# Pairing VectorE's residual adds in the second half of three RMS borders of a two-block transformer kernel

## The chip, the cores and the metric

The program runs on one core of a Trainium2 chip. The metric is the device time of one execution in microseconds. A core has a matrix engine (TensorE, PE in the profile), a vector engine (VectorE, DVE), an activation engine (ScalarE, ACT), GpSimd (POOL) and a sync engine (SP) that issues transfers. Each has its own instruction stream, and they meet by semaphores. PEld is the weight load that goes with each matmul.

## What is computed

The reference runs three layers over 512 tokens of width 1024, all in float32. What matters here is the residual border between a branch `m` and what follows it, three times in the first block:

```python
def _rms_norm(x, g):
    y = x * lax.rsqrt(jnp.mean(x * x, axis=-1, keepdims=True) + NORM_EPS)
    return y * g

h = h + _rms_norm(m, norm_g[layer, 1])                                     # a border
f = _squared_relu_mlp(_rms_norm(h, norm_g[layer, 2]), ffn_w1[layer], ffn_w2[layer])
h = h + _rms_norm(f, norm_g[layer, 3])                                     # a border
```

The borders in question are the one between the first mixer and the first feed-forward part (`ffn0`), the one between `ffn0` and the second mixer (`sgu_in`), and the one between the second mixer and the second feed-forward part (`ffn1`).

## The kernel before

Activations lie transposed: feature on the 128 partitions, in 8 blocks `k` of 128 features, tokens along the free axis. `h` is the residual stream, `acc` the branch's result, both 128 x 8 x 512 float32. A border works on the tokens in two halves `s` of 256, so that TensorE can go on with one half while the other is being normalised.

Products are made in three passes, for precision: each operand is split into a high part (rounded for the matmul) and a low part (the rest). The high part of the next stage's input, `xa[:, k, 0]`, is made by ScalarE from `h` with the gain of the next norm; the low part, `xa[:, k, 1]`, is made by VectorE from `h` and the high part. The reciprocal root of the next norm is applied later, so TensorE needs only these two.

In the second half (s = 1) of a border, the work for each block k before the change is:

1. VectorE, line 596 (`dve_post_scale`): `acc = acc * gain * rs`, where `rs` lies in a PSUM bank (the reciprocal of line 593). It raises `post_ready`.
2. VectorE, line 601 (`dve_post_add`): waits for `post_ready` of its block, `h = h + acc`. It raises `h_ready`.
3. ScalarE, line 637 (`hi` in `act_boundary`): waits for `h_ready` to reach the block's count, writes the high part of `xa`, raises `pre_hi`.
4. VectorE, line 610 (`lo` in `dve_boundary`): waits for `pre_hi`, writes the low part, raises `pre_lo`.
5. TensorE: at the borders into `ffn0` and `ffn1` line 510 (`pe_quad`), 12 products of 128x256 for each block: four for the high part with the weights' high part, four for the high part with the weights' low part, and then, after a wait for `pre_lo`, four for the low part. At the border into `sgu_in` line 1754 (`v_first`), 6 products of 128x512 for each block, two, two and two in the same order. The high part is waited for with `pre_hi` at each block's first product.

Ahead of block 0 of the second half TensorE runs a few products on constants (line 482, `pe_hold`; 3 at the first and third border, 4 at the second), whose result is not used.

VectorE's order is written out by hand in the table `STEPS`: "rs" is the reciprocal, ("step", k) is scale k, add k, low part k - 1, "last" is low part 7, and "split" is the low part of a weight panel (line 365). ScalarE's order, in `act_boundary`, is high parts 0 to 6, the high part of panel 4, high part 7, and the high parts of panels 5 and 6. Behind the half comes the panel work of the next stage (line 392 at `ffn0` and `ffn1`, line 1766 at `sgu_in`).

Of the kernel before, what the change touches and what calls it, by code (L numbers as in the profile page):

```python
# [24 lines left out]
ALU = mybir.AluOpType  # L25
# [7 lines left out]
KC = D // P  # L33
# [185 lines left out]
def build(nc, stream, x, vec, con, rope, cmp_pos, cmp_w1, cmp_w2, gate_w, w_s, b_s, rpb, mask, out, stop=None):  # L219
    with ExitStack() as ctx:  # L220
        sems = {}

        def sem(name):
            if name not in sems:
                sems[name] = ctx.enter_context(nc.semaphore(name))
            return sems[name]
# [4 lines left out]
        def keep(name, shape, dt=F32):  # L231
            size = int(np.prod(shape[1:])) * (2 if dt == BF16 else 4)
            size = -(-size // 128) * 128
            t = nc.alloc_sbuf_tensor_at(name, shape, dt, offset=place[0])
            place[0] += size
            return t

        h = keep("h", [P, KC, T])
# [9 lines left out]
        rs = keep("rs", [P, T])  # L248
# [13 lines left out]
        def at(name, shape, kb, dt=F32):  # L262
            assert shared + int(kb * 1024) + int(np.prod(shape[1:])) * 4 <= nc.sbuf_usable_end, name
            return nc.alloc_sbuf_tensor_at(name, shape, dt, offset=shared + int(kb * 1024))

        xb = at("xb", [P, KC, 2, T], 0, F32R)
        acc = at("acc", [P, KC, T], 32)
# [69 lines left out]
        def col(table, i=0):  # L337
            return vecs[:, VEC[table] + i:VEC[table] + i + 1]
# [21 lines left out]
        def dve_split(dve, n, more=0):  # L360
            m = n + AHEAD
            if m >= NP:
                return
            dve.wait_ge(hi_done, m + 1 + more)
            nc.vector.tensor_tensor(ring[:, m % RING, 1], raw[:, m % RING], ring[:, m % RING, 0].bitcast(F32),  # L365
                                    ALU.subtract).then_inc(lo_done, 1)
# [59 lines left out]
        def half(s):  # L426
            return slice(HT * s, HT * s + HT)
# [14 lines left out]
        def pe_squares(pe, i):  # L442
# [6 lines left out]
        STEPS = ([("rs", 0), ("step", 0), ("out", 0), ("step", 1), ("split", 0), ("step", 2), ("out", 1), ("step", 3),  # L449
                  ("out", 2), ("out", 3), ("split", 1), ("step", 4), ("step", 5), ("split", 2), ("step", 6), ("split", 3),  # L450
                  ("step", 7), ("last", 0)],
                 [("rs", 1)] + [("step", k) for k in range(8)] + [("last", 1), ("split", 4), ("split", 5), ("split", 6)])

        def tail_base(name):
            return BASE[name] + dict(STAGES)[name] - 4, TAIL_AT[name]
# [135 lines left out]
        def dve_post_rs(dve, chain, r, s):  # L591
            dve.wait_ge(sem("post_sd"), 2 * r + s + 1)
            chain(nc.vector.reciprocal(ps[6 + s][:, half(s)], ps[6 + s][:, half(s)]))

        def dve_post_scale(dve, r, s, k, g):
            nc.vector.scalar_tensor_tensor(out=acc[:, k, half(s)], in0=acc[:, k, half(s)], scalar=col("norm_g", g * KC + k),
                                           in1=ps[6 + s][:, half(s)], op0=ALU.mult, op1=ALU.mult).then_inc(sem("post_ready"), 1)

        def dve_post_add(dve, r, s, k):
            dve.wait_ge(sem("post_ready"), 16 * r + 8 * s + k + 1)  # L600
            nc.vector.tensor_tensor(h[:, k, half(s)], h[:, k, half(s)], acc[:, k, half(s)], ALU.add)\
                .then_inc(sem("h_ready"), 1)

        def dve_boundary(dve, chain, r, g_post, name, g_pre, out):

            u0 = 8 + 16 * r

            def lo(s, k):
                dve.wait_ge(sem("pre_hi"), u0 + 8 * s + k + 1)
                nc.vector.scalar_tensor_tensor(out=xa[:, k, 1, half(s)], in0=h[:, k, half(s)],  # L610
                                               scalar=col("norm_g", g_pre * KC + k),
                                               in1=xa[:, k, 0, half(s)].bitcast(F32), op0=ALU.mult, op1=ALU.subtract)\
                    .then_inc(sem("pre_lo"), 1)

            for q in range(4):
                out(0, q)
            for s in range(2):
                for what, i in STEPS[s]:
                    if what == "rs":
                        dve_post_rs(dve, chain, r, s)  # L620
                    elif what == "step":
                        dve_post_scale(dve, r, s, i, g_post)
                        dve_post_add(dve, r, s, i)
                        if i >= 1:
                            lo(s, i - 1)
                    elif what == "last":
                        lo(s, KC - 1)
                    elif what == "out":
                        out(1, i)
                    else:  # L630
                        dve_split(dve, BASE[name] + i - AHEAD)
# [1718 lines left out]
        def _(dve):  # L2350
# [327 lines left out]
            dve_split(dve, BASE["mix0_nsa"])  # L2678
            dve.wait_ge(taken["act"], READS["act"][BASE["mix0_nsa"]])
            dve_boundary(dve, chain, 0, 1, "ffn0", 2, out_nsa)  # L2680
            dve_ffn(dve, "ffn0")
            dve_boundary(dve, chain, 1, 3, "sgu_in", 4, out_tail("ffn0"))
            for k in range(1, KC):
                dve.wait_ge(sem("pre_sq"), k + 1)
# [90 lines left out]
            for j in range(13):  # L2775
                dve_split(dve, B + j)
                if j % 2 == 1:
                    dve.wait_ge(panel_done, B + j + 1)
                    nc.vector.tensor_copy(acc[:, j // 2], ps[BANK[B + j]][:, :]).then_inc(taken["dve"], 2)
            dve_boundary(dve, chain, 2, 5, "ffn1", 6, out_sgu)  # L2780
            dve_ffn(dve, "ffn1")

# [278 lines left out]
```

## Time and profile before

| what | value |
|---|---|
| time, median of 3 runs | 2045.3 us (2044.89 to 2045.57) |
| the profiled execution's own time | 2045.47 us |
| its span, first to last instruction | 2043.7 us |
| busy: TensorE, VectorE, ScalarE, GpSimd | 99%, 51%, 39%, 8% |
| mean granted TensorE clock | 0.999 of full speed |
| the chain that ended last: TensorE, VectorE, ScalarE | 93%, 4%, 2% |

The profiled execution's time is its span and 1.8 us around it. A share of busy time is a mean over all stages. How the engines stand in one short stretch, such as a border of some 12 us, is read from the timeline of that stretch.

### The profile page before, as it was taken

To read this page: it belongs to the slowest core of one execution; us is meant where nothing else is said; L and a number is where in the kernel's file an instruction comes from. 1 tells how busy PE (TensorE), PEld (TensorE's weight loads), DVE (VectorE), ACT (ScalarE), POOL (GpSimd) and SP (SyncE) were. 2 spreads that over 40 slices of the span, in tenths; PEclk is the share of its full clock that TensorE was granted. 3 is DMA by queue.
4 is the path that set the end of the run, shared out by engine and by line. 5 is a ranking of instruction groups with operands and counts; after the bars stand their busy time and mean duration, and the time that the engine had idled before them with its cause. 6 is when DMAs were issued, how large, how long until landed. Compare 5 with 4: busy or idle time off the path is not lost.

```text
span 2043.7 us, 28848 instructions
## 1 busy us (share of the span) xinstructions
PE 2022.7 (99%) x11240; PEld 1711.4 (84%) x11240; DVE 1048.1 (51%) x1722; ACT 802.4 (39%) x1348; POOL 173.6 (8%) x160
## 2 busy tenths in 40 slices
PE   9999999999999999999999999999999999999998
PEld 7888788888889888889888888987888898888887
DVE  6557867344345736527443434727544545344344
ACT  7326644223233533324332323535554345323232
POOL 1001010100002001210220002300000220000000
PEclk9999999999999999999999999999999999999999
DMA  5222013332322322232333323232122313333321
GB/s 194 89 71 84 22 38 108 93 103 92 97 89 86 120 86 86 87 103 73 104 93 102 98 88 103 83 113 93 44 63 83 103 52 114 93 95 94 99 83 42
DMA packets 52047, 182.12 MB, mean 89 GB/s; under 512 B 5872, under 2 KB 8064, under 8 KB 51936
## 3 DMA queue, kind: packets, MB, share of 16 engines
q1 hardware_dynamic: 50112, 173.23, 27.0%
q0 software_dynamic: 1824, 7.32, 1.0%
q8 instruction: 80, 1.31, 0.3%
q14 instruction: 31, 0.25, 0.0%
HBM read 178.43 MB, written 2.10 MB: 88 GB/s over the span
## 4 chain that ended last, share of the span: by engine, by line
PE 93%; DVE 4%; ACT 2%; issue 0%; DMA 0%; POOL 0%; SPq 0%; ACTq 0%; DVEq 0%
PE ps L392 59%; PE ps L1101 5%; PE ps L471 4%; PE ps L510 3%; PE ps L1766 3%; PE ps L1843 3%; PE ps L1041 2%; PE ps L1084 2%; PE ps L1058 1%; PE ps L1754 1%; PE ps L1486 1%; PE ps L822 1%; PE ps L1464 1%; PE ps L1602 1%; DVE ring L365 1%; PE ps L1856 1%
## 5 line engine op out<-in xcount | busy, mean ns | idle before, releaser
L392 PE MATMUL ps<-xa,ring 128*128 128x512 f32 x3048 | 702.9, 391 | 0.0
L392 PEld LDWEIGHTS ps<-xa,ring 128*128 128x128 f32 x3048 | 570.1, 188 | 120.5 <-issue 2.7
L358 ACT ACTIVATE ring<-raw 128x1024 fp32r<-128x1024 f32 x320 | 336.6, 1054 | 482.2 <-PE ps L392 382.1
L365 DVE TENSOR_TENSOR ring<-raw,ring 128x1024 fp32r<-128x1024 f32 x320 | 402.0, 1259 | 205.5 <-ACT ring L358 205.0
L392 PE MATMUL ps<-xb,ring 128*128 128x512 f32 x2208 | 502.6, 389 | 0.0
L392 PEld LDWEIGHTS ps<-xb,ring 128*128 128x128 f32 x2208 | 414.4, 188 | 86.1
L947 DVE TENSOR_TENSOR ffsq<-relu 128x512 f32<-128x512 f32 x96 | 66.3, 691 | 178.8 <-ACT relu L906 178.8
L964 DVE TENSOR_TENSOR acc<-acc,ps 128x512 f32<-128x512 f32 x68 | 46.8, 688 | 196.3 <-PE ps L392 196.3
L906 ACT ACTIVATE relu<-ps 128x512 f32<-128x512 f32 x64 | 38.1, 596 | 185.0 <-PE ps L392 182.7
L950 DVE TENSOR_TENSOR xb<-ffsq,xb 128x512 fp32r<-128x512 f32 x96 | 66.5, 692 | 75.8 <-ACT xb L898 75.8
L1101 PE MATMUL ps<-xa,ring 128*128 128x512 f32 x432 | 104.3, 396 | 0.0
L510 PE MATMUL ps<-xa,ring 128*128 128x256 f32 x768 | 97.1, 286 | 2.5 <-issue 1.2
L510 PEld LDWEIGHTS ps<-xa,ring 128*128 128x128 f32 x768 | 93.7, 192 | 5.1 <-issue 1.4
L1101 PEld LDWEIGHTS ps<-xa,ring 128*128 128x128 f32 x432 | 79.4, 188 | 18.2
L471 PE MATMUL ps<-xb,ring 128*128 128x256 f32 x576 | 71.6, 285 | 0.0
L471 PEld LDWEIGHTS ps<-xb,ring 128*128 128x128 f32 x576 | 70.3, 192 | 0.5
L1766 PE MATMUL ps<-ring,xa 128*128 128x512 f32 x288 | 65.7, 389 | 0.0
L898 ACT ACTIVATE xb<-ffsq 128x512 fp32r<-128x512 f32 x96 | 59.8, 623 | 10.4 <-DVE ffsq L947 10.3
L1766 PEld LDWEIGHTS ps<-ring,xa 128*128 128x128 f32 x288 | 54.0, 188 | 11.2
L1843 PE MATMUL ps<-yhi,ring 128*128 128x512 f32 x192 | 59.4, 389 | 0.0
L906 ACT ACTIVATE relu<-ps,vecs 128x512 f32<-128x512 f32 x32 | 22.0, 686 | 88.1 <-PE ps L392 86.7
L563 POOL TENSOR_TENSOR part<-part,xf 128x512 f32<-128x512 f32 x8 | 14.4, 1801 | 473.5 <-ACT xf L547 473.5
(371 smaller groups left out, 2061.2 us busy)
## 6 DMA issues: line engine op xcount, KB each, us to landing
raw<-in_stream SPq DMA_DIRECT2D x320, 512.0 KB, 3.5
t<-in_rpb POOLq DMA_DIRECT2D x8, 384.0 KB, 5.6
h<-in_x SPq DMA_DIRECT2D x8, 256.0 KB, 7.1
c_w<-in_cmp_w POOLq DMA_DIRECT2D x4, 512.0 KB, 4.0
out_y<-h SPq DMA_DIRECT2D x16, 128.0 KB, 1.9
cons<-in_con SPq DMA_DIRECT2D x1, 578.0 KB, 8.9
raw<-in_stream SPq DMA_DIRECT2D x2, 256.0 KB, 3.9
wst<-in_w_s POOLq DMA_DIRECT2D x1, 512.0 KB, 3.5
```

The costliest lines, as they stand in the source:

```text
L358: nc.scalar.activation(ring[:, m % RING, 0], raw[:, m % RING], ACT.Copy).then_inc(hi_done, 1)
L365: nc.vector.tensor_tensor(ring[:, m % RING, 1], raw[:, m % RING], ring[:, m % RING, 0].bitcast(F32), ALU.subtract).then_inc(lo_done, 1)
L392: mm = nc.tensor.matmul(bank[:, :], ring[:, n % RING, w, k * P:(k + 1) * P], operand[:, k, xx], start=(start and i == 0 and w == 0 and xx ...
L471: mm = nc.tensor.matmul(ps[bank][:, half(q % 2)], ring[:, n % RING, w, k * P:(k + 1) * P], operand[:, k, xx, half(s)], start=(k == 0 and w ...
L510: mm = nc.tensor.matmul(ps[QUAD[c]][:, half(s)], ring[:, (n0 + k // 2) % RING, w, at_w:at_w + P], xa[:, k, xx, half(s)], start=(k == 0 and ...
L898: nc.scalar.activation(xb[:, j - 1, 0], ffsq[:, (j - 1) % 2], ACT.Copy).then_inc(sem("ff_hi"), 1)
L906: nc.scalar.activation(relu[:, j % 2], ps[at][:, :], ACT.Relu, bias=b).then_inc(taken["act"], 1)
L947: nc.vector.tensor_tensor(ffsq[:, j % 2], relu[:, j % 2], relu[:, j % 2], ALU.mult)\
L950: nc.vector.tensor_tensor(xb[:, j, 1], ffsq[:, j % 2], xb[:, j, 0].bitcast(F32), ALU.subtract).then_inc(sem("ff_lo"), 1)
L1101: mm = nc.tensor.matmul(ps[BANK[n]][:, :], ring[:, n % RING, w, k * P:(k + 1) * P], operand[:, k, xx], start=(k == 0 and w == 0 and xx == ...
L1766: mm = nc.tensor.matmul(ps[V_BANKS[g][t]][:, :], xa[:, k, xx, t * P:(t + 1) * P], ring[:, n % RING, w, (k % 2) * T:(k % 2) * T + T], start ...
L1843: mm = nc.tensor.matmul(ps[BANK[n]][:, :].rearrange("p (t d) -> p t d", t=TB), ring[:, n % RING, w, k * P:(k + 1) * P], y_block(KC * i + k ...
```

## The change

In the second half of each of the three borders, the table now lists ("two", k) for k = 0, 2, 4, 6 in place of the eight ("step", k). A "two" scales blocks k and k + 1, adds both to `h` in one instruction of 128 x 2 x 256 that waits for both scales and raises `h_ready` by 2, and then makes the low parts k - 2 and k - 1, if there are any. "last" of the second half makes low parts 6 and 7. The first half, ScalarE's order and TensorE's order are as they were.

```diff
-                 [("rs", 1)] + [("step", k) for k in range(8)] + [("last", 1), ("split", 4), ("split", 5), ("split", 6)])
+                 [("rs", 1)] + [("two", k) for k in range(0, 8, 2)] + [("last", 1), ("split", 4), ("split", 5), ("split", 6)])
...
+        def dve_post_add_two(dve, r, s, k):
+            dve.wait_ge(sem("post_ready"), 16 * r + 8 * s + k + 2)
+            nc.vector.tensor_tensor(h[:, k:k + 2, half(s)], h[:, k:k + 2, half(s)], acc[:, k:k + 2, half(s)], ALU.add)\
+                .then_inc(sem("h_ready"), 2)
...
+                    elif what == "two":
+                        dve_post_scale(dve, r, s, i, g_post)
+                        dve_post_scale(dve, r, s, i + 1, g_post)
+                        dve_post_add_two(dve, r, s, i)
+                        if i >= 2:
+                            lo(s, i - 2)
+                            lo(s, i - 1)
                     elif what == "last":
+                        if s == 1:
+                            lo(s, KC - 2)
                         lo(s, KC - 1)
```

VectorE at the start of the second half of the first border, before. L596 is the scale, L601 the add, L610 the low part:

```order
L596 SCALAR_TENSOR_TENSOR acc<-acc,vecs,ps 128x256 [waits dve_chain]
L601 TENSOR_TENSOR h<-h,acc 128x256 [waits post_ready]
L596 SCALAR_TENSOR_TENSOR acc<-acc,vecs,ps 128x256
L601 TENSOR_TENSOR h<-h,acc 128x256 [waits post_ready]
L610 SCALAR_TENSOR_TENSOR xa<-h,vecs,xa 128x256 [waits pre_hi]
```

The last three rows repeat for blocks 2 to 7. The same place in the changed kernel, where line 606 is the two-block add and line 615 the low part:

```order
L596 SCALAR_TENSOR_TENSOR acc<-acc,vecs,ps 128x256 [waits dve_chain]
L596 SCALAR_TENSOR_TENSOR acc<-acc,vecs,ps 128x256
L606 TENSOR_TENSOR h<-h,acc 128x2x256 [waits post_ready]
L596 SCALAR_TENSOR_TENSOR acc<-acc,vecs,ps 128x256 x2
L606 TENSOR_TENSOR h<-h,acc 128x2x256 [waits post_ready]
L615 SCALAR_TENSOR_TENSOR xa<-h,vecs,xa 128x256 [waits pre_hi] x2
```

What moved: the first `h` of the half comes after two scales and a two-block add; the first low part comes after four scales and two two-block adds, where it came after two scales and two adds.

TensorE at the same place has the same rows in both kernels, the constants' products and then blocks 0 and 1:

```order
L482 MATMUL ps<-cons 128x256 x3
L510 MATMUL ps<-xa,ring 128x256 [waits pre_hi]
L510 MATMUL ps<-xa,ring 128x256 x7
L510 MATMUL ps<-xa,ring 128x256 [waits pre_lo]
L510 MATMUL ps<-xa,ring 128x256 x3
```

Nothing moved there: a block's first eight products need its high part alone, and the last four need its low part.

## Rows read from the trace of the kernel before

**Rows 1.** The page: granted clock in its 40 slices, and the chain's shares.

```profile
PEclk9999999999999999999999999999999999999999
...
PE 93%; DVE 4%; ACT 2%; issue 0%; DMA 0%; POOL 0%; SPq 0%; ACTq 0%; DVEq 0%
```

**Rows 2.** VectorE's timeline, first border: start, us, engine, line, operation.

```profile
309.97 0.48 DVE L596 SCALAR_TENSOR_TENSOR acc<-acc,vecs,ps 128x256 f32<-128x256 f32 x1
310.49 0.42 DVE L601 TENSOR_TENSOR h<-h,acc 128x256 f32<-128x256 f32 x1
310.83 0.47 DVE L596 SCALAR_TENSOR_TENSOR acc<-acc,vecs,ps 128x256 f32<-128x256 f32 x1
...
311.68 0.48 DVE L610 SCALAR_TENSOR_TENSOR xa<-h,vecs,xa 128x256 fp32r<-128x256 f32 x1
312.07 0.47 DVE L596 SCALAR_TENSOR_TENSOR acc<-acc,vecs,ps 128x256 f32<-128x256 f32 x1
...
313.32 0.48 DVE L596 SCALAR_TENSOR_TENSOR acc<-acc,vecs,ps 128x256 f32<-128x256 f32 x1
```

**Rows 3.** ScalarE's timeline, first border, high parts 0 and 6 and a panel.

```profile
310.94 0.51 ACT L637 ACTIVATE xa<-h,vecs 128x256 fp32r<-128x256 f32 x1 [3.20 <-DVE h L601]
...
318.03 0.51 ACT L637 ACTIVATE xa<-h,vecs 128x256 fp32r<-128x256 f32 x1 [0.73 <-DVE h L601]
318.45 1.04 ACT L358 ACTIVATE ring<-raw 128x1024 fp32r<-128x1024 f32 x1
```

**Rows 4.** TensorE's timeline, first border.

```profile
309.95 1.46 PE L482 MATMUL ps<-cons 128*128 128x256 f32 x6
311.50 11.77 PE L510 MATMUL ps<-xa,ring 128*128 128x256 f32 x96
323.12 13.11 PE L392 MATMUL ps<-xa,ring 128*128 128x512 f32 x57
```

**Rows 5.** VectorE's timeline, second border: scale 0.

```profile
665.70 0.48 DVE L596 SCALAR_TENSOR_TENSOR acc<-acc,vecs,ps 128x256 f32<-128x256 f32 x1
```

**Rows 6.** The chain at the second border: start, us, what.

```profile
667.23 11.19 PE ps L1754 x48
678.42 5.67 PE ps L1766 x25
```

**Rows 7.** The chain at the third border.

```profile
950.39 0.49 DVE acc L596
...
951.93 11.78 PE ps L510 x96
963.71 6.37 PE ps L392 x28
```

**Rows 8.** Adds by line: min/median/max ns, first and last start, forms.

```profile
L601 DVE TENSOR_TENSOR h<-h,acc x48: 424/425/462, 290.0 to 959.2; 128x256 f32<-128x256 f32 x48
...
L540 DVE TENSOR_TENSOR acc<-acc,ps x12: 673/687/689, 635.5 to 2027.1; 128x512 f32<-128x512 f32 x12
```

**Rows 9.** VectorE's timeline in ffn0: an operation of 512 columns and its successor.

```profile
334.22 0.69 DVE L950 TENSOR_TENSOR xb<-ffsq,xb 128x512 fp32r<-128x512 f32 x1 [0.70 <-ACT xb L898]
334.83 1.22 DVE L365 TENSOR_TENSOR ring<-raw,ring 128x1024 fp32r<-128x1024 f32 x1
```

**Rows 10.** Timeline, second border: a low part, and TensorE's load waiting for it.

```profile
662.85 0.48 DVE L610 SCALAR_TENSOR_TENSOR xa<-h,vecs,xa 128x256 fp32r<-128x256 f32 x1
...
663.38 1.67 PEld L1754 LDWEIGHTS ps<-ring,xa 128*128 128x128 f32 x8 [0.19 <-DVE xa L610]
```

**Rows 11.** TensorE's timeline, first border, first half: waits before products.

```profile
295.82 3.58 PE L510 MATMUL ps<-xa,ring 128*128 128x256 f32 x28 [1.21 <-issue]
299.88 1.22 PE L510 MATMUL ps<-xa,ring 128*128 128x256 f32 x8 [0.47 <-DVE ring L365]
```

**Rows 12.** Stretches: us, PE busy (products), granted clock, DMA share, GB/s.

```profile
294.60:302.00 7.40, 5.46 (x40) 1.00 0.32 95
...
311.50:323.20 11.70, 11.70 (x97) 1.00 0.05 6
```

## The prediction, made before the changed kernel ran

> **What bounds the kernel now.** The page comes first. TensorE holds 93% of the chain that ended last, at a granted clock that is full in every slice [rows 1]. Anything that makes TensorE start later lengthens the kernel by as much, unless it would have waited for something else anyway. Next I looked at the stretch that the change touches, the second half of each border, engine by engine on the timeline. VectorE works there with hardly a gap: scale, add, low part, and block 2's scale starts 1.25 us before block 3's (312.07 and 313.32) [rows 2]. TensorE starts that half at 311.50 and then runs 96 products in 11.77 us with no gap up to the next stage [rows 4]. That is 0.1226 us for a product and 1.47 us for a block of 12. So the half has two limits, one after the other. Its start hangs on VectorE and ScalarE: reciprocal, scale 0, add 0, high part 0, first product (311.45 is the high part's end, 311.50 the product's start) [rows 2 to 4]. After the start the limit is TensorE, since a block takes it 1.47 us and VectorE 1.25 us. The other two borders look the same: 48 products in 11.19 us, 0.233 us each, at the second [rows 6], 96 in 11.78 us at the third, where the chain itself goes through scale 0 [rows 7].
>
> **What the change removes.** Four adds in each border's second half. One add of 256 columns takes 0.425 us. One of 512 columns, of the same two-row pattern of 2 x 256 (line 540 addresses two blocks of `acc` like that, with its second input in PSUM), takes 0.687 us [rows 8]. An operation with both inputs in SBUF takes 0.69 us, and its successor starts 0.61 us after it [rows 9]. I take 0.69 us for the pair and 0.61 us to the next start. Between small operations: an unheld one follows a scale or a low part after 0.39 us (311.68 to 312.07), an add follows a scale that it waits for after 0.50 to 0.52 us, and what follows a small add comes after 0.34 us [rows 2]. A pair of blocks costs VectorE 2 x 1.25 = 2.50 us before. It costs 0.39 + 0.51 + 0.61 + 0.39 + 0.39 = 2.29 us after. That is 0.21 us less for a pair and 0.8 us for a border. This time is off the path, because TensorE takes 2.94 us for a pair. So it is priced at nothing, and what hides it is the 0.44 us per pair by which VectorE was ahead already.
>
> **What it adds, first term: the half starts later.** Count from scale 0 at 309.97. Before, add 0 starts at 310.49 and ends at 310.91. The high part starts at 310.94, 0.03 us on [rows 2, 3]. After: scale 1 at 310.36, the pair's add at 310.87, its end at 311.56, high part 0 at 311.59 for 0.51 us, its end at 312.10, and the first product at 312.15. That is 0.65 us later than 311.50. The reciprocal ahead of it doesn't move, since nothing before it is changed. At the second border the same chain gives scale 0 plus 1.53 us before (665.70 to 667.23) [rows 5, 6] and plus 2.18 us after, at the third plus 1.54 us before (950.39 to 951.93) [rows 7]. Each pays 0.65 us. The products on constants don't hide it: they end before 311.50 in both cases [rows 4].
>
> **Second term: the first low part comes later still.** After the first pair's add at 310.87 come scale 2 at 311.48, scale 3 at 311.87, the second pair's add at 312.38, and only then low part 0 at 312.99. It ends at 313.47. TensorE starts 0.05 us after a low part that it waits for (662.85 + 0.48, and 663.38) [rows 10], so at 313.52. TensorE's first eight products need the high part alone and take 8 x 0.1226 = 0.98 us, to 313.13. It then waits 0.39 us. Before, low part 0 ended at 312.16 [rows 2] against a need at 312.48, so there was no wait. At the second border four products of 0.233 us stand ahead of the low part: need at scale 0 plus 3.11 us, there at plus 3.55 us, a wait of 0.44 us.
>
> **Does more wait behind it?** Block 1 starts at 314.01 and needs its low part at 314.99; it is ready at 313.38 + 0.48 = 313.86. Block 2 starts at 315.48; its high part is made at 313.10 to 313.61, its low part (scales 4 and 5, add, then the low part at 315.28) ends at 315.76 against a need at 316.46. From there VectorE gains 0.65 us a pair. So the two first waits are all. High part 1 follows high part 0 by about 0.42 us, as the panel's work follows high part 6 (318.03 to 318.45) [rows 3], and is done before block 1 wants it. ScalarE's panel splits and VectorE's (line 365) come no later than before, since the last pair's add comes earlier than add 7 did.
>
> **Sum.** 0.65 + 0.39 = 1.04 us at the first and third border, 0.65 + 0.44 = 1.09 us at the second: 3.17 us. Behind each half TensorE goes on without a gap into the next stage [rows 4, 6, 7], so all of it reaches the end. The profiled execution took 2045.47 us, which makes 2048.64. It stands 0.17 us above the median of the runs, so the forecast for a median is 2048.5 us, 0.15% slower. Bounds: the start by 0.60 to 0.70 us and the low part's wait by 0.25 to 0.5 us, whatever the pair's exact pace, give 2.6 to 3.6 us, or 2047.9 to 2048.9 us.
>
> **Rivals.** *The pair costs as much as two adds.* The new form, two inputs and an output all in SBUF and all in two pieces, has no row of its own. Were it 2 x 0.425 = 0.85 us, each pair's add would be 0.16 us longer: the high part comes 0.16 us later and low part 0 0.32 us later, as it stands behind two such adds. Three borders pay 0.96 us more: 2049.5 us, slower by over 0.2% from an add of some 0.84 us on. Against it stands the 0.687 us of a form with two of its three operands in two pieces [rows 8]. Chance 0.08.
>
> *The clock falls.* TensorE now idles about 0.7 us before the half and 0.4 us inside it. In the first half of the same border it idles 1.21 us and 0.47 us, and the granted clock is 1.00 in that stretch and in the second half [rows 11, 12]. That is the upper of its two levels, 2.4 GHz. At the lower one, 1.2 GHz, a product's 0.12 us would be doubled: eight products at the lower level in one border (8 x 0.1226 = 0.98 us) would take the total past 0.2%, and a whole half would give some 2060 us. Chance 0.03. The Trainium skill (TensorE: Matmul & The Clock Gate, Part 1) says that an idle array falls back to the half clock, which speaks against this change; the trace shows longer waits than the new ones without a fall.
>
> *Only the start pays.* If TensorE's restart is slow enough, or the low parts quick enough, that low part 0 is there in time, the sum is 3 x 0.65 = 1.95 us: 2047.2 us. It needs 0.39 us of error in a chain of seven steps. Chance 0.09.
>
> *Not slower: the delay is swallowed.* If TensorE waited soon behind the half for something that doesn't move, a transfer or a panel, it would lose nothing: 2045.3 us. It needs over a microsecond of such waits behind each border, and no gap stands there [rows 4, 6, 7]. Chance 0.04.
>
> *Faster: VectorE's saving is the path.* If the second half ran at VectorE's pace, twelve adds fewer, at 2 x 0.425 - 0.687 = 0.163 us each, would give 1.96 us: 2043.3 us. It needs a block to take TensorE less than 1.25 us, and it takes 1.47 us. Chance 0.02. The Trainium skill (VectorE: DVE Perf Modes, the section on the TRN2 errata) says that the fixed part is paid once by a large tile and again by each small one, and advises 512 elements or more; the trace agrees on the durations (0.425 and 0.687 us) [rows 8], and whoever goes by that rule alone forecasts this gain.
>
> **The numbers.** The forecast has the other 0.74. A measurement of this kernel tells about 0.2%, 4.1 us, from no change, so slower by over 0.2% means above 2049.4 us. That takes most of the first rival, the clock, and a small tail of the forecast: 0.10. Faster by over 0.2% would be under 2041.2 us: 0.01. Within: 0.89. The range from 2047.1 to 2049.4 us holds the forecast and the case in which only the start pays, and leaves out the clock, the two cases at or under no change, most of the double-priced add and a thin tail of the forecast, some 0.15 to 0.2.
>
> **What the profile of the changed kernel would show.** First step: TensorE's last gap before line 510 of the second half at 2.2 us after scale 0 where it is 1.5 us now, with ScalarE's high part as releaser. Second step: a second gap of 0.4 us eight products later, with the low part as releaser. The pair's add: 12 rows of about 0.69 us. VectorE's rows of the half close up: pairs 2.3 us apart, and the last low part done slightly earlier. Granted clock 1.00 at all three. I'd be wrong if the second gap is missing, if a third follows (block 1 or 2 waits as well), or if TensorE's start of the next stage moves by something other than 1.0 us a border.

## The result, and the profile after

| | before | changed |
|---|---|---|
| median, 14 runs each | 2045.72 us | 2049.14 us |
| ratio of the changed kernel to before, 95% interval | | 1.0018 (1.0011 to 1.0025) |
| the profiled execution's span | 2043.7 us | 2047.3 us |

The change costs 3.4 us by the medians, 3.6 us by the spans of the two profiles. It is slower beyond its interval, and the interval reaches over 0.2%. In some executions of both kernels the mean granted clock is 0.997 instead of 0.999 and the time about 2 us longer (in the trace of `low_ahead`, one of these, the granted clock is 0.97 in the first 50 us and 1.00 at all three borders), so small differences are read below from the time between two events of one border, and medians "at full clock" are over executions with a clock of 0.999.

On the page of the changed kernel VectorE is busy 1.5 us less than before (1048.1 us before), with 12 instructions fewer:

```profile
PE 2023.5 (99%) x11240; PEld 1711.5 (84%) x11240; DVE 1046.6 (51%) x1710; ACT 802.2 (39%) x1348; POOL 173.6 (8%) x160
...
PE 91%; DVE 6%; ACT 2%; issue 1%; DMA 0%; POOL 0%; ACTq 0%; DVEq 0%
```

The chain's share has moved from TensorE to VectorE: 93% and 4% in [rows 1], 91% and 6% here. That is more than the 3.6 us lost, and it is no measure of them. At the second border the chain before the change stays on TensorE through the first half; now it leaves TensorE at 645.22 us and runs through VectorE's queue of the first half, more than 20 us, up to scale 0 at 666.79, although that queue takes as long as it did (20.12 us from its reciprocal to scale 0, 20.13 before). The timeline of the first border shows what was lost, VectorE, ScalarE and TensorE together (start, us, engine, line, in brackets the idle time and its releaser). It answers to [rows 2 to 4]:

```profile
309.86 0.87 DVE L596 SCALAR_TENSOR_TENSOR acc<-acc,vecs,ps 128x256 f32<-128x256 f32 x2
310.84 0.69 DVE L606 TENSOR_TENSOR h<-h,acc 128x512 f32<-128x512 f32 x1
311.44 0.87 DVE L596 SCALAR_TENSOR_TENSOR acc<-acc,vecs,ps 128x256 f32<-128x256 f32 x2
311.56 0.91 ACT L651 ACTIVATE xa<-h,vecs 128x256 fp32r<-128x256 f32 x2 [3.93 <-DVE h L606]
...
312.12 1.22 PE L510 MATMUL ps<-xa,ring 128*128 128x256 f32 x8 [0.83 <-ACT xa L651]
312.42 0.69 DVE L606 TENSOR_TENSOR h<-h,acc 128x512 f32<-128x512 f32 x1
313.03 0.87 DVE L615 SCALAR_TENSOR_TENSOR xa<-h,vecs,xa 128x256 fp32r<-128x256 f32 x2
...
313.56 10.70 PE L510 MATMUL ps<-xa,ring 128*128 128x256 f32 x87 [0.21 <-DVE xa L615]
```

TensorE's 96 products stood in one row in [rows 4]. They are now in two: eight, then a wait for `xa` from line 615, the low part, then the rest. The first product comes at 312.12, 2.26 us after scale 0 (309.86), where it was 1.53 us. After the eight products TensorE resumes at 313.56, 3.70 us after scale 0. An idle time in brackets is counted from the modelled end of the last product, so it is shorter than what the stall costs. The starts of the single products give that: they stand 0.12 us apart, but the second product after a wait comes some 0.22 us after the first (311.50 and 311.73 before the change). Product 9 would have come at 2.26 + 0.22 + 7 x 0.12 = 3.32 us after scale 0. It came 0.38 us later, and the new start takes another 0.10 us: 0.48 us in all.

The measure that I use from here on is the time from scale 0 of the second half to the first product of the next stage. The product's row at the first border of the changed kernel, for one:

```profile
324.22 4.95 PE L392 MATMUL ps<-xa,ring 128*128 128x512 f32 x21
```

| from scale 0 to the next stage, us | border 1 | border 2 | border 3 | sum of the differences |
|---|---|---|---|---|
| before | 13.15 | 12.56 | 13.16 | |
| changed | 14.36 (+1.21) | 13.85 (+1.29) | 14.35 (+1.19) | +3.69 |

That is the whole loss; nothing came back behind the borders and nothing was added. The spans differ by 0.1 us less, because in this execution scale 0 of the first border, ahead of anything that was changed, came 0.11 us earlier (309.86 against 309.97).

### The profile page after: what moved, and what is told of

Same layout as the page of the kernel before. It is cut to its first block, busy times and chain, and to the rows that moved or that the text cites. A ratio compares the mean times of both kernels' runs of the same rounds, so it can differ in the third digit from the quotient of the medians.

```text
span 2047.3 us, 28848 instructions
## 1 busy us (share of the span) xinstructions
PE 2023.5 (99%) x11240; PEld 1711.5 (84%) x11240; DVE 1046.6 (51%) x1710; ACT 802.2 (39%) x1348; POOL 173.6 (8%) x160
## 3 DMA queue, kind: packets, MB, share of 16 engines
q8 instruction: 80, 1.31, 0.3%
## 4 chain that ended last, share of the span: by engine, by line
PE 91%; DVE 6%; ACT 2%; issue 1%; DMA 0%; POOL 0%; ACTq 0%; DVEq 0%
PE ps L392 59%; PE ps L1115 5%; PE ps L471 4%; PE ps L510 3%; PE ps L1780 3%; PE ps L1857 3%; PE ps L1055 2%; PE ps L1098 2%; PE ps L1072 1%; PE ps L1500 1%; PE ps L836 1%; DVE ring L365 1%; PE ps L1478 1%; PE ps L1616 1%; DVE acc L596 1%; PE ps L1870 1%
```

## The experiments

Each is run against the kernel before, with 11 runs of its own where nothing else is said. I held three theories. A: the half is late by its first low part. B: by its late start, the high part. C: VectorE's busy time counts. All edits are to the second half's list in the table, if nothing else is said; they are written short, in the table's words, and a "-" line stands for the changed kernel, from which all versions were made. "scale", "add", "add2" (the two-block add) and "low" are its words.

### The pairs kept, the low parts ahead of the add: `low_ahead`

```diff
-two: scale k, scale k+1, add2 k, low k-2, low k-1
+two: scale k, scale k+1, low k-2, low k-1, add2 k
```

> The pairs' adds stay as in the changed kernel, but within each pair the two low parts of the pair before go ahead of the add: scale 2, scale 3, low 0, low 1, add of 2 and 3. Theory A (the half is late by its first low part, TensorE resumes 3.70 us after scale 0 in the changed kernel): low 0 starts 2.4 us after scale 0 instead of 3.2, is ready before TensorE wants it at 3.24, and only the high part's delay of 0.73 us a border is left: 2.2 us slower than before in all, one gap of TensorE at each border. Theory B (the pair's add costs through the high part alone, and the low part's wait is incidental): no better than the changed kernel, 3.6 us slower than before. Theory C (VectorE's busy time is the path): 1.9 us faster than before.

Measured: ratio 1.0008 (0.9999 to 1.0017), full-clock median 2047.0 us against 2045.0 us. By the border: +0.73, +0.72, +0.72, sum 2.17 us. TensorE has one gap and then all 96 products in one piece:

```profile
312.33 0.87 DVE L596 SCALAR_TENSOR_TENSOR acc<-acc,vecs,ps 128x256 f32<-128x256 f32 x2
...
314.59 11.66 PE L510 MATMUL ps<-xa,ring 128*128 128x256 f32 x95 [0.83 <-ACT xa L659]
```

The first product is 2.26 us after scale 0, as in the changed kernel, and the second wait is gone. So of 3.7 us the low part's place holds 1.5, and with the low part in time the late high part costs 2.2. Theory C, which has the same number of instructions to save, is out.

### An early high part and a late low part: `low_late`

```diff
-scale 0, scale 1, add2 0, scale 2, scale 3, add2 2, low 0, low 1, ...
+scale 0, add 0, scale 1, add 1, scale 2, scale 3, add2 2, low 0, low 1, ...
```

> Blocks 0 and 1 are scaled and added singly as in the kernel before, so that the high part of block 0 is as early as there, but low parts 0 and 1 come only after the pair's add of blocks 2 and 3. Pairs for blocks 2 to 7. Theory A (the first low part's lateness decides and holds the first term in it): TensorE starts 1.53 us after scale 0 and then waits for low 0 until 3.84, needed at 2.51: 1.33 us at the first and third border, 1.38 us at the second, 4.0 us slower than before, more than the changed kernel though the half starts 0.73 us earlier. Theory B (the late high part is the main cost): 3 x 0.4 = 1.2 us slower or less.

Measured: ratio 1.0020 (1.0011 to 1.0030). By the border +1.31, +1.37, +1.32, sum 4.00 us, which is the 4.0 of theory A and more than the changed kernel's 3.69. TensorE at the first border, where scale 0 starts at 309.55:

```profile
311.08 1.22 PE L510 MATMUL ps<-xa,ring 128*128 128x256 f32 x8
313.37 10.81 PE L510 MATMUL ps<-xa,ring 128*128 128x256 f32 x88 [1.06 <-DVE xa L615]
```

The half starts at 1.53 us as before the change, 0.73 us ahead of the changed kernel, and ends 0.1 us later than there, since the first low part frees it at 3.82 us. Theory B is out as the cause of the whole. The two terms of my sum are no two costs: the start counts only where the low part is in time.

### The changed order with single adds: `single_adds`

```diff
-add2 k
+add k, add k+1   (each waits for both scales)
```

> The changed kernel's order with each two-block add split back into two single adds, both of which wait for both scales. It tells why the pair's add starts 0.98 us after the first scale where 0.90 was forecast. If the wait behind two overlapped scales is slow, add 0 starts at 0.98 too, low 0 is ready at 3.86 us after scale 0, and the kernel is 4.1 us slower than before, 0.5 us more than the changed kernel, though the high part comes 0.27 us earlier than there. If the two-row form is slow to start, add 0 starts at 0.90, low 0 is ready at 3.70, and it is 3.6 us slower, as the changed kernel. If the high part decided, it would be 0.8 us better than the changed kernel.

Measured: ratio 1.0018 (1.0009 to 1.0028); by the border +1.21, +1.29, +1.18, sum 3.68 us, the second branch of the expectation. The first product is there 1.93 us after scale 0, a third of a microsecond before the changed kernel's, and the half ends with it to the hundredth:

```profile
309.90 0.87 DVE L596 SCALAR_TENSOR_TENSOR acc<-acc,vecs,ps 128x256 f32<-128x256 f32 x2
310.81 0.76 DVE L601 TENSOR_TENSOR h<-h,acc 128x256 f32<-128x256 f32 x2
311.49 0.87 DVE L596 SCALAR_TENSOR_TENSOR acc<-acc,vecs,ps 128x256 f32<-128x256 f32 x2
...
313.61 10.81 PE L510 MATMUL ps<-xa,ring 128*128 128x256 f32 x88 [0.56 <-DVE xa L615]
```

Two single adds start 0.91 us after scale 0 and occupy VectorE until 1.59 us; the two-block add starts at 0.98 us and lets the next scale go at 1.58 us. What the pair saves (0.61 against 0.68 us) it loses at its start. So beside single adds in the same order the merged add bought VectorE nothing, and all of the loss comes from the order that the merging asked for.

### Two more products on constants: `hold_two_more`

```diff
-HOLD = {"ffn0": (0, 3), "ffn1": (0, 3), ...
+HOLD = {"ffn0": (0, 5), "ffn1": (0, 5), ...
-pe_hold(pe, ps[V_BANKS[0][2]][:, half(0)], 4)
+pe_hold(pe, ps[V_BANKS[0][2]][:, half(0)], 6)
```

> The changed kernel with two more products on constants (0.49 us each) ahead of each second half, so that TensorE's wait of 0.8 us before the first product is filled and the first product comes about 0.15 us later at the first border. Theory A (what decides is when low part 0 is there): no change against the changed kernel within 0.2 us, 3.6 us slower than before, TensorE's second gap shrinks by what the first product is late. Theory B (the start of the half decides): 0.3 to 0.5 us slower than the changed kernel. If the gaps cost through TensorE's clock, filling one would make it faster than the changed kernel.

Measured: ratio 1.0017 (1.0008 to 1.0026); by the border +1.20, +1.26, +1.19. The first product came at 2.26 us after scale 0 (309.59 and 311.85): the 0.86 us of extra products just fitted into the wait, so it was not late at all, and this run tells A from B less than I had wanted. What it does tell is that filling TensorE's longest wait brings nothing, so the waits cost no clock. The clock is granted in full in the changed kernel's three borders too (PEclk, the figure behind the products; then DMA share and GB/s):

```profile
306.00:324.20 18.20, 17.15 (x136) 1.00 0.23 74
663.00:680.60 17.60, 16.61 (x72) 1.00 0.36 124
948.00:966.00 18.00, 16.74 (x132) 1.00 0.23 64
```

### Pairs only for the later blocks: `pairs_from_4` and `pairs_from_2`

```diff
 pairs_from_4: scale 0, add 0, then scale k, add k, low k-1 for k = 1, 2, 3, then
+scale 4, scale 5, add2 4, low 3, scale 6, scale 7, add2 6, low 4, low 5, low 6, low 7
 pairs_from_2: scale 0, add 0, scale 1, add 1, low 0, then
+scale 2, scale 3, add2 2, low 1, scale 4, scale 5, add2 4, low 2, low 3, scale 6, scale 7, add2 6, low 4, ..., low 7
```

> Blocks 0 to 3 singly as before, blocks 4 to 7 in pairs. By the time of block 4 TensorE is behind VectorE: low part 3 is ready at 6.8 us after scale 0 against a need at 6.9, high part 4 at 6.9 against 7.4. Theory A (only what TensorE waits for early in the half costs): the time of before within 0.2 us, no gap of TensorE after its first product. If VectorE's busy time were on the path, six adds fewer would give 1.0 us; if a pair cost by itself, half of the changed kernel's loss, 1.8 us slower.

> Blocks 0 and 1 singly with low part 0 where it was, blocks 2 to 7 in pairs. Low part 1 now comes after the pair's add of blocks 2 and 3: ready 4.2 us after scale 0 (4.3 if the add behind two scales starts 0.07 us late again) against a need at 3.98 at the first and third border and at 3.86 at the second. Theory A: waits of 0.3, 0.4 and 0.3 us, 1.0 us slower than before in all. Without a low part's part in it: the time of before.

Measured: `pairs_from_4` 1.0009 (1.0000 to 1.0018), +0.43, +0.81, +0.43 by the border, sum 1.67 us; `pairs_from_2` 1.0014 (1.0005 to 1.0023), +0.82, +1.04, +0.81, sum 2.67 us. Both are slower than I had expected, and for one reason: I had followed one low part to its need and not the next. In `pairs_from_4` low part 3 is close to in time, but low 4 stands behind the add of 6 and 7, and that is what TensorE waits for:

```profile
311.64 0.48 DVE L596 SCALAR_TENSOR_TENSOR acc<-acc,vecs,ps 128x256 f32<-128x256 f32 x1
...
319.19 0.69 DVE L606 TENSOR_TENSOR h<-h,acc 128x512 f32<-128x512 f32 x1
319.80 1.27 DVE L615 SCALAR_TENSOR_TENSOR xa<-h,vecs,xa 128x256 fp32r<-128x256 f32 x3
...
320.33 5.06 PE L510 MATMUL ps<-xa,ring 128*128 128x256 f32 x40 [0.19 <-DVE xa L615]
```

Low 4 starts 8.16 us after scale 0 and is needed at 1.53 + 0.22 + 55 x 0.12 = 8.35; it ends at 8.64 and frees the product at 8.69, 0.34 us late, and the new start adds 0.10. In `pairs_from_2` the expected wait is there: low 1 frees product 21 at 4.22 us where its turn was at 4.03, which with the new start is 0.29 us, against 0.3 expected. What was not expected stands behind it: low 2, behind the add of 4 and 5, frees product 33 at 6.20 us (310.09 and 316.29), another 0.44 and 0.10 us. The mechanism holds (the releaser is a low part in each); the expectation was wrong on `pairs_from_4`, which was to have no wait, and left one of two out in `pairs_from_2`. It shows too that even late in the half, where VectorE is a good microsecond ahead, a low part cannot stand behind one more pair.

### The change at one border: `one_border`

```diff
-for what, i in STEPS[s]:
+for what, i in (SINGLE if s == 1 and r > 0 else STEPS[s]):
```

> The change at the first border alone, the other two as before. Theory A: a third of the loss, 1.2 us slower than before; nothing that is lost at one border comes back or grows later.

Measured: ratio 1.0008 (0.9999 to 1.0017). By the border +1.21 us at the first, +0.01 and -0.02 at the others. A third of the loss per border, and nothing of it returns.

### Where the two-block add's late start is from: `two_row_singles` and `three_forms`

```diff
 two_row_singles, the kernel before but for the form of the second half's adds:
-h[:, k, half(s)] + acc[:, k, half(s)]
+two = [t[:, k, half(s)].rearrange("p (b a) -> p a b", a=2) for t in (h, acc)]
 three_forms, in dve_post_add_two:
+r == 0: two adds of h[:, k:k + 2, 128 columns];  r == 1: two single adds, one wait for both scales each
+r == 2: the two-block add, with a wait for k + 1 ahead of that for k + 2
```

> The kernel before with the second half's single adds written as two interleaved rows of 128 columns, all else alike. It tells whether the two-row form of an add is what starts 0.07 us late behind a scale that it waits for (the two-block add started 0.98 us after its first scale, the single add in the same place 0.91). If the form does it, each add starts 0.58 us after its scale instead of 0.51, the half's first product comes 0.07 us later and VectorE's step is 1.32 us instead of 1.25, still under TensorE's 1.47: 0.2 us slower than before. If it is the size of 512 columns or the pairing, adds start at 0.51 and nothing moves.

> The changed kernel with the pair's adds in another form at each border, to tell why the two-block add starts 0.98 us after the first of its two scales where 0.90 was forecast, and a single add in its place 0.91. First border: two adds of 2 x 128 columns, each over both blocks, so the rows lie a block apart but the size is 256. Second border: two single adds, each with one wait for both scales. Third border: the two-block add with a wait for the first scale ahead of its wait for both. Read from the timeline, start of the add after the first scale. If rows that lie a block apart are slow to start behind a scale just ended, 0.98, 0.91 and 0.98 us. If it is the single wait for two scales, 0.98, 0.98 and 0.91. If it needs both rows and 512 columns, 0.91, 0.91, 0.98. The time is that of the changed kernel within 0.5 us in all cases.

Measured: `two_row_singles` 1.0000 (0.9991 to 1.0009), its adds start 0.52 us after their scale (312.43 and 312.95), as single rows do. `three_forms` (10 runs) 1.0021 (1.0011 to 1.0031), adds at 0.91, 0.90 and 1.01 us after scale 0. Neither two rows a block apart, nor a wait for two scales, is what makes it late. By the expectation's three branches it would be two rows of 256 together, but these branches left out what the form also changes: it raises its semaphore by 2. The chain of waits shows what the lateness is (start, us, what). First the changed kernel, then the third border of `three_forms`:

```profile
309.86 0.88 DVE acc L596 x2
310.74 0.03 issue
310.77 0.02 DVEq L605
310.79 0.04 issue
310.84 0.69 DVE h L606
```

```profile
952.55 0.89 DVE acc L596 x2
953.44 0.03 issue
953.47 0.05 DVEq L619
953.51 0.04 issue
953.56 0.69 DVE h L620
```

DVEq is VectorE's own queue, and line 605 is the `wait_ge` itself. The two-block add's wait runs as an instruction of its own ahead of the add, and 0.10 us lie between scale 1's end and the add, where 0.03 us lie between a scale and a single add. With two waits it takes 0.12 us. The single adds of `two_row_singles`, `three_forms` and `single_adds` show no such piece.

The first border of `three_forms` tells what separates the wait. Line 609 runs there twice for each pair, two adds of one shape, 2 x 128 columns, each with one `wait_ge`. The first raises its semaphore by 1, the second raises `h_ready` by 2. Of the eight adds, four have their wait as an instruction of the queue (line 608), and each stands ahead of a second add (the rows by line: count, duration in ns as min/median/max, first and last start, forms):

```profile
L608 DVEq EVENT_SEMAPHORE  x4: 21/21/21, 310.6 to 316.9; - x4
...
L609 DVE TENSOR_TENSOR h<-h,acc x8: 415/422/426, 310.6 to 317.3; 128x256 f32<-128x256 f32 x8
```

The kernel before has the same pair of cases on one line elsewhere. Line 1181 is a tiny operation in one row, which waits for the reduction just ahead of it and raises its semaphore by 1 or by 2. The eight that raise it by 2 are those of 128x2, and eight waits stand apart (line 407). The row of those waits, then the timeline of one of either case:

```profile
L407 DVEq EVENT_SEMAPHORE  x8: 21/21/21, 1452.3 to 1530.2; - x8
...
1442.11 0.56 DVE L1174 TENSOR_REDUCE stat<-ps 128x1 f32<-128x384 f32 x1 [0.50 <-PE ps L1047]
1442.70 0.16 DVE L1181 TENSOR_TENSOR stat<-stat 128x1 f32<-128x1 f32 x1
...
1477.37 0.76 DVE L1174 TENSOR_REDUCE stat<-ps 128x1 f32<-128x256 f32 x2 [4.14 <-PE ps L1041]
1478.23 0.16 DVE L1181 TENSOR_TENSOR stat<-stat 128x2 f32<-128x2 f32 x1
```

The one that raises by 1 starts 0.03 us after the reduction's end, the one that raises by 2 starts 0.10 us after it, the same two values as for a single add and for the pair's. Of VectorE's operations that wait and raise a semaphore by more than 1, 20 in the kernel before and 32 in the changed one, none carries its wait itself. So the lateness comes from raising `h_ready` by 2 and not from the add's shape. A two-block add that raises by 1, with ScalarE's waits counted to match, wasn't run; by these rows it would start 0.07 us earlier.

### What VectorE's queue in the first half is worth: `first_half_pair`, `rs_early`, `interleaved`

All three keep the second half as it was before the change.

```diff
 first_half_pair, first half:
-step 4, step 5, split 2, step 6
+scale 4, scale 5, add2 4, low 3, split 2, low 4, step 6
 rs_early, and 1 product on constants in place of 3, 4 and 3:
-first half: ..., step 7, last 0            second half: rs 1, step 0, ...
+first half: ..., step 7, rs 1, low 7       second half: step 0, ...
 interleaved, as rs_early, and in the first half from block 4:
+scale 4, low 3, add 4, scale 5, split 2, add 5, low 4, scale 6, low 5, add 6, scale 7, split 3, add 7, low 6, rs 1, low 7
```

> The second half as before. In the first half of each border blocks 4 and 5 are scaled and added as a pair (scale 4, scale 5, add of both, low 3, panel split, low 4). There VectorE is the bound: everything up to the second half's scale 0 hangs on its queue, and TensorE has over 1 us of slack on blocks 4 and 5. Theory A: what VectorE saves, some 0.05 to 0.1 us a border, moves scale 0 of the second half and the start of TensorE's half forward: 0.1 to 0.3 us faster than before. A rival: the saving is lost in a later wait of VectorE for ScalarE, the time of before.

> The second half as before, but its reciprocal (1.69 us of VectorE) goes ahead of the first half's last low part, where VectorE waited 0.2 us for ScalarE, and the products on constants are cut from 3, 4 and 3 to one at each border. If scale 0 of the second half is what the half's start hangs on, it comes 0.38 us earlier and so does the first product: 1.1 us faster than before. TensorE waits 0.3 to 0.5 us for the first half's last low part, which the fewer products on constants make room for. Rival: that wait eats the gain, or fewer constants' products cost clock: the time of before or slower.

> As rs_early, and in the first half's blocks 4 to 7 each add stands behind some other operation (a low part or a panel split) instead of right behind the scale that it waits for, which hides 0.11 us a block: scale 4, low 3, add 4, scale 5, split 2, add 5, low 4, scale 6, low 5, add 6, scale 7, split 3, add 7, low 6, reciprocal, low 7. If VectorE's queue up to scale 0 of the second half is the path, scale 0 comes some 0.8 to 1.2 us earlier, and the half starts as soon as TensorE is through with the first: 0.6 to 1.0 us a border, 2 to 3 us faster than before. Rival: a late high part 5 or split 3 makes TensorE wait in the first half, which takes the gain back.

Measured: `first_half_pair` 0.9996 (0.9987 to 1.0005) and `rs_early` 0.9997 (0.9988 to 1.0006), both not told from no change by their runs. `interleaved` 0.9987 (0.9978 to 0.9996), median 2043.48 us against 2045.58 us, and at full clock 2043.2 against 2045.35: 2.1 us faster than before, the one version whose interval lies clear of no change on the faster side. Its VectorE rows at the third border, block 6 and then from add 7 of the first half on, and TensorE's start:

```profile
944.58 0.47 DVE L595 SCALAR_TENSOR_TENSOR acc<-acc,vecs,ps 128x256 f32<-128x256 f32 x1
944.97 0.48 DVE L614 SCALAR_TENSOR_TENSOR xa<-h,vecs,xa 128x256 fp32r<-128x256 f32 x1
945.36 0.42 DVE L600 TENSOR_TENSOR h<-h,acc 128x256 f32<-128x256 f32 x1
...
947.29 0.42 DVE L600 TENSOR_TENSOR h<-h,acc 128x256 f32<-128x256 f32 x1
947.62 0.48 DVE L614 SCALAR_TENSOR_TENSOR xa<-h,vecs,xa 128x256 fp32r<-128x256 f32 x1
948.02 1.76 DVE L592 RECIPROCAL ps<-ps 128x256 f32<-128x256 f32 x1
949.81 0.48 DVE L614 SCALAR_TENSOR_TENSOR xa<-h,vecs,xa 128x256 fp32r<-128x256 f32 x1
950.21 0.47 DVE L595 SCALAR_TENSOR_TENSOR acc<-acc,vecs,ps 128x256 f32<-128x256 f32 x1
...
951.74 2.53 PE L509 MATMUL ps<-xa,ring 128*128 128x256 f32 x19 [0.22 <-ACT xa L658]
```

The reciprocal fills the time in which the last low part would wait for ScalarE, and an add no longer stands right behind its scale: it starts 0.39 us after the low part ahead of it instead of 0.51 us after its scale. The 2.1 us are the lower end of the 2 to 3 us that were expected.

The traces divide them, by the time from the first half's reciprocal to the first product of the next stage:

| us, from the first half's reciprocal to the next stage | border 1 | border 2 | border 3 | sum of the differences |
|---|---|---|---|---|
| before | 35.47 | 32.71 | 32.17 | |
| `first_half_pair` | 35.29 | 32.54 | 32.02 | -0.50 |
| `rs_early` | 35.22 | 32.41 | 31.89 | -0.83 |
| `interleaved` | 34.88 | 31.99 | 31.52 | -1.96 |

So the earlier reciprocal is worth 0.8 us and the interleaving another 1.1 us. `rs_early` was expected to bring 1.1 us. The products on constants have no part in it: in all four kernels the half's first product comes 1.52 to 1.54 us after scale 0. The pair in the first half did gain, by 0.17 us a border: scale 6 comes 3.50 us after scale 4 at the third border, where it was 3.66 us. Where VectorE's queue is the path the saving counts, and it needs no merging, since single adds in the pair's order hold VectorE as long (see `single_adds`).

## Why the prediction was right and wrong

The direction and the mechanism were right: slower by 0.15% was forecast, 0.17% to 0.18% was measured, and 2049.14 us lies inside the range, near its upper end. The size was too small: 1.0 us a border was forecast, and anything else was named as a sign of being wrong; 1.2 to 1.3 us was measured. The two waits stand where they were put, the first with ScalarE's high part as releaser, the second eight products later with the low part as releaser, no third one follows, and the granted clock is full. The rest by its steps:

- **What the change removes.** Off the path, as said. 12 adds fewer make VectorE 1.5 us less busy (1.96 had been reckoned). The pair's duration of 0.69 us was right to the hundredth (0.692 us in twelve rows), and so the rival of a doubly priced add is out.
- **The first term** was put at 0.65 us and measured 0.73 us (2.26 against 1.53). The step that failed is the pair's add "at 310.87", 0.90 us after scale 0. It started 0.98 us after it. I had taken the start of an add behind a scale that it waits for from single adds (0.50 to 0.52 us), and this add, which raises its semaphore by 2, has its wait as an instruction of its own in the queue.
- **The second term.** Low part 0 was put at 3.02 us after scale 0 and came at 3.17. Two pair's adds stand ahead of it, each late by 0.075 us. TensorE's wait was put at 0.39 and 0.44 us and costs 0.48 us at the first border and 0.52 at the second. It was also worked out from a mean of 0.1226 us a product, in which the 0.10 us of one start are spread over 96 products; the second start that the wait brings was not priced.
- **The sum.** 3.17 us forecast, and 0.15 us for each of three borders is 0.45 us: 3.62 us, against 3.69 us by the borders. The pair's late start, once in the first term and twice in the second's low part, is nearly all that was missing; the rest is some 0.02 us a border from the pace of the products and their second start.
- **The chances** were too narrow. 0.89 stood on "within 0.2%", with a forecast 0.9 us under that bound and a form of instruction that had no row in the trace. The first rival named that lack and priced the add's length; the cost was at its start. A ratio of 1.0018 with an interval up to 1.0025 is no clear case of "within".
- **A side claim.** VectorE's and ScalarE's panel splits were to come no later than before. ScalarE's third one now waits for a product of the half and starts at 321.60 us, some 0.85 us later than before, and VectorE's third one waits for it (322.69). At these borders that cost nothing: behind the half TensorE's rows run on as before.
- **What the sum hid.** The text adds a late start and a late low part as if each were a cost. The runs show one cost: TensorE's half ends at the low part's arrival plus what is left of the products, 3.70 us after scale 0 here. `single_adds` starts the half 0.33 us earlier and ends it at the same time; `low_late` starts it 0.73 us earlier and ends it later. Whoever had repaired only the high part would have won nothing.

## What to carry to other kernels

When two engines pass blocks through a chain, write down for each block when the consumer needs each of its parts, and check every one of them against the new order, not the first alone; twice here a block behind the one that had been checked was the late one. A merged instruction can save its fixed part only where that engine is the bound, and it delays whatever was fed by the first of the two; feed the consumer's first block singly, and let what the consumer already has cover the pair. Raise a semaphore by 1 where the operation waits for its direct predecessor: raising by 2 put the start 0.07 us later here, each time. Where an in-order engine is the bound, an operation that waits for its direct predecessor is worth less than one with something useful between the two: that (1.1 us), together with the earlier reciprocal (0.8 us), and not the merging, gave 2 us.

## What the runs showed of the hardware

- An operation of VectorE that raises its semaphore by more than 1 has its wait as an instruction of the queue of its own: the pair's add (12 of 12), the second adds of 2 x 128 in `three_forms` (4 of 4, and none of the 4 of the same shape that raise by 1), line 1181 in the kernel before (8 of 8, and none of the 16 that raise by 1). Where it waits for its direct predecessor, 0.10 us lie between that one's end and its start, against 0.03 us; with two waits 0.12 us.
- An add that waits for the scale right ahead of it starts 0.51 us after the start of that scale. With another operation of the same length between the two, it starts 0.39 us after the start of that one (945.36 behind 944.97 in `interleaved`).
- TensorE's products of 256 columns stand 0.12 us apart, and the second one behind a wait comes some 0.22 us after the first (312.12 and 312.35, 313.56 and 313.78 at the first border of the changed kernel). So each further wait inside a half costs 0.10 us more than its idle time.
- The fixed cost of an add is lower in the queue than in its duration: two adds of 256 last 2 x 0.425 = 0.85 us, but the second starts 0.34 us after the first, and together they hold VectorE for 0.68 us against 0.61 us for one of 512. A saving reckoned from durations (0.163 us an add) is more than twice the one that the starts show (0.07 us).
- TensorE's waits in these stretches, up to 1.05 us by the brackets of its rows at the third border, left the granted clock at 1.00.
